# A shorter step table for the state-space heads: 43 steps in place of 45, at lower paces

## The reference, cut to what matters

```python
cs = jnp.cumsum(dA, axis=2)
lmat = segsum_exp(jnp.moveaxis(cs, 2, -1))            # exp(cs_i - cs_j), i >= j
cb = jnp.einsum('bclgn,bcsgn->bcgls', cm, bm)
y_diag = jnp.einsum('bcgls,bcgrls,bcsgrp->bclgrp', cb, lmat, xdt)
decay_states = jnp.exp(cs[:, :, -1:] - cs)
states = jnp.einsum('bclgn,bclgr,bclgrp->bcgrpn', bm, decay_states, xdt)
...
y_off = jnp.einsum('bclgn,bcgrpn,bclgr->bclgrp', cm, states_in, jnp.exp(cs))
return (y_diag + y_off).reshape(b, length, g, r, p)
```

```python
y = ssd_chunked(...) + xs_h * d_skip
y = y.reshape(b, length, SSM_D_INNER) * jax.nn.silu(z)
yg = y.reshape(b, length, SSM_GROUPS, SSM_NORM_GROUP)
yg = yg * lax.rsqrt(jnp.mean(yg * yg, axis=-1, keepdims=True) + RMS_EPS)
y_ssm = (yg * norm_w) @ w_out_ssm
```

## Time and profile before

| | |
|---|---|
| runs | 3578.57, 3582.47, 3583.49 us |
| profiled execution | 3578.57 us, span 3576.4 us, so 2.2 us lie around the span |
| instructions | 38935 |
| PE busy | 3362.9 us (94%) |
| PEld busy | 2729.3 us (76%) |
| DVE busy | 1723.0 us (48%) |
| ACT busy | 1340.7 us (37%) |
| mean granted PE clock | 0.973 |
| DMA | 288.05 MB, 81 GB/s on average |

### The profile page before, as it was taken

How to read it: one execution, slowest core, us unless ns; L and a number is a source line. 1 busy time by engine, 2 the same in 40 slices (tenths; PEclk the granted TensorE clock), 3 DMA queues, 4 the chain that set the end, 5 groups by cost and what they waited for, 6 DMA issues and landing times.

```text
span 3576.4 us, 38935 instructions
## 1 busy us (share of the span) xinstructions
PE 3362.9 (94%) x15366; PEld 2729.3 (76%) x15366; DVE 1723.0 (48%) x2415; ACT 1340.7 (37%) x1898; POOL 30.6 (1%) x62
## 2 busy tenths in 40 slices
PE   8999988799999999998888999999999998999998
PEld 6888765587888888876657788877777876778887
DVE  4443444654443444344555544455455566544443
ACT  4332334443332333233443333335454466433322
POOL 0000000000000000000000000000000000000000
PEclk9999999999999999999989999999999998999999
DMA  4333211112333232321211332321111222333332
GB/s 140 95 97 96 90 65 53 33 36 94 94 97 94 93 100 93 97 88 62 68 28 30 94 100 93 98 79 53 62 62 51 83 85 67 94 99 99 96 93 66
DMA packets 107396, 288.05 MB, mean 81 GB/s; under 512 B 22912, under 2 KB 34176, under 8 KB 107216
## 3 DMA queue, kind: packets, MB, share of 16 engines
q1 hardware_dynamic: 91696, 278.70, 24.9%
q10 hardware_dynamic: 14208, 2.63, 0.4%
q0 software_dynamic: 1312, 4.25, 0.4%
HBM read 282.64 MB, written 2.88 MB: 80 GB/s over the span
## 4 chain that ended last, share of the span: by engine, by line
PE 77%; DVE 11%; ACT 8%; issue 3%; DMA 1%; ACTq 0%; DVEq 0%; SPq 0%
PE ps L722 23%; PE ps L724 22%; PE ps L723 22%; DVE wl L1830 3%; ACT wh L1289 3%; DVE mf L2014 2%; PE ps L731 2%; PE ps L1029 1%; PE ps L1024 1%; PE ps L1185 1%; DVE mf L2024 1%; PE ps L736 1%; PE ps L1167 1%; PE ps L1181 0%; ACTq L1564 0%
## 5 line engine op out<-in xcount | busy, mean ns | idle before, releaser
L1830 DVE TENSOR_TENSOR wl<-raw,wh 128x1024 fp32r<-128x1024 f32 (+2 forms) x581 | 652.3, 1123 | 1421.9 <-ACT wh L1289 1420.2
L722 PE MATMUL ps<-hnh,wh 128*128 128x512 f32 x2712 | 1097.1, 405 | 40.9 <-DVE mf L2478 16.6
L723 PE MATMUL ps<-hnl,wh 128*128 128x512 f32 x2712 | 1071.6, 395 | 0.0
L724 PE MATMUL ps<-hnh,wl 128*128 128x512 f32 x2712 | 1070.9, 395 | 0.0
L1289 ACT ACTIVATE wh<-raw 128x1024 fp32r<-128x1024 f32 (+2 forms) x581 | 567.2, 977 | 1067.6 <-PE ps L724 1046.4
L722 PEld LDWEIGHTS ps<-hnh,wh 128*128 128x128 f32 x2712 | 520.6, 192 | 173.3 <-issue 25.2
L724 PEld LDWEIGHTS ps<-hnh,wl 128*128 128x128 f32 x2712 | 518.5, 191 | 111.6
L723 PEld LDWEIGHTS ps<-hnl,wh 128*128 128x128 f32 x2712 | 520.5, 192 | 109.0 <-issue 4.0
L722 PE MATMUL ps<-mr,wh 128*128 128x512 f32 x1300 | 512.4, 394 | 22.9 <-DVE h L1956 9.3
L724 PE MATMUL ps<-mr,wl 128*128 128x512 f32 x1300 | 507.4, 390 | 0.0
L723 PE MATMUL ps<-mr,wh 128*128 128x512 f32 x1300 | 507.3, 390 | 0.0
(11 more groups left out here) (324 smaller groups left out, 2537.9 us busy)
## 6 DMA issues: line engine op xcount, KB each, us to landing
raw<-in_w_in SPq DMA_DIRECT2D x140, 512.0 KB, 3.5
raw<-in_ffn_w_gate SPq DMA_DIRECT2D x88, 512.0 KB, 3.5
raw<-in_ffn_w_up SPq DMA_DIRECT2D x88, 512.0 KB, 3.5
raw<-in_ffn_w_down SPq DMA_DIRECT2D x64, 512.0 KB, 3.5
raw<-in_w_ffn_in SPq DMA_DIRECT2D x44, 512.0 KB, 3.5
raw<-in_ffn_w_down SPq DMA_DIRECT2D x32, 384.0 KB, 3.1
raw<-in_w_out SPq DMA_DIRECT2D x32, 256.0 KB, 2.7
raw<-in_w_out_ssm SPq DMA_DIRECT2D x32, 256.0 KB, 2.6
```

The lines of the kernel that those rows point to most:

```text
L722: self.e.matmul(out, ah, bh, start=start, stop=False, skip_group_check=shared)
L723: self.e.matmul(out, ah, bl, start=False, stop=False, skip_group_check=shared)
L724: m = self.e.matmul(out, al, bh, start=False, stop=stop, skip_group_check=shared)
L1830: self.e.tensor_tensor(lo[:, 0:n], k.raw[u % NRAW][:, 0:n], hi[:, 0:n].bitcast(F), ALU.subtract).then_inc(k.w_lo, 1)
```

## The change

The table of steps becomes two steps shorter and the four paces become lower, so that the steps still fill about the same blocks. The second pair of turns moves from step 10 to step 8. The arguments and all that follows from them move two steps forward (arguments 8 to 6, exponentials 9 to 7, `w` 10 to 8, values 14 to 12). The four x steps, which were 8, 9, 12 and 13, are 8, 9, 10 and 11. The states and the part between chunks move four steps forward (16 to 12), `y` and `z` two (18 to 16), root, diagonal and results two. The work itself, its instructions and their data, is the same.

```diff
-PACE_SSM_ROWS, PACE_SSM, PACE_LRU, PACE_LRU_END = 1.1, (1.15, 0.86, 0.86, 0.95), 0.65, 1.0
+PACE_SSM_ROWS, PACE_SSM, PACE_LRU, PACE_LRU_END = 1.1, (1.1, 0.82, 0.82, 0.9), 0.65, 1.0
...
-SSM_STEPS, SCAN_STEPS = 45, 11
-AT_CB, AT_TURN, AT_X = (0, 2, 2, 3), (6, 10), (8, 9, 12, 13)
-AT_ARG, AT_EXP, AT_W, AT_V = 8, 9, 10, 14
-AT_ST, AT_OFF, AT_Y = 16, 16, 18
-AT_ROOT, AT_RESULT, AT_HIGH, AT_LOW = (32, 34, 36), (39, 39, 39, 39), (40, 41, 42, 43), (41, 42, 43, 44)
+SSM_STEPS, SCAN_STEPS = 43, 11
+AT_CB, AT_TURN, AT_X = (0, 2, 2, 3), (6, 8), 8
+AT_ARG, AT_EXP, AT_W, AT_V = 6, 7, 8, 12
+AT_ST, AT_OFF, AT_Y = 12, 12, 16
+AT_ROOT, AT_RESULT, AT_HIGH, AT_LOW = (30, 32, 34), (37, 37, 37, 37), (38, 39, 40, 41), (39, 40, 41, 42)
...
-            four_at("x", AT_X), [(AT_ST + 2 + 4 * c, f"{n}{c}") for c in (1, 2) for n in "ds"],
+            [(AT_X + i, f"x{i}") for i in range(4)], [(AT_ST + 2 + 4 * c, f"{n}{c}") for c in (1, 2) for n in "ds"],
...
-            if t in AT_X:
-                i = AT_X.index(t)
+            if AT_X <= t < AT_X + 4:
+                i = t - AT_X
```

## The result

The changed kernel takes 3609.4 us (median of four, 3607.68 to 3610.8), the kernel before beside it 3580.74. The ratio is 1.0080, 95% interval 1.0062 to 1.0097. I had predicted 3597 us, +0.40%, with a range of 3584 to 3604. The sign was right, the size half of what came, and the time lies outside the range.

A forecast was written before the change was run, and what follows sets the result against it. PE bounds the kernel, nearly every instruction in the head groups being on the path. Added 19.25 us less removed 4.85 gave net +14.4: 3593.0 us for the profiled execution, 3597 as median (+0.40%), range 3584 to 3604.

The forecast's parts named there:

- the clock term: Behind turn 3's waits in groups 1 to 3, PE runs at lower clock: 3 x 1.65 = 4.95 us, bounds 0 and 7.
- turn 3 on x1, groups 1 to 3: PE waits at turn 3 for x1, now behind w0 on DVE: 3 x 3.2 = 9.7 us, plus 4.95 of clock.
- n0 on x3, groups 1 and 2: PE waits at n0 for x3, now behind a wl on DVE: 1.4 us twice, 2.8 us, no clock loss.
- turn 0 on CB, groups 2 and 3: Turn 0 stands one block nearer to ACT's copy of CB: 0.4 us in group 2, 0.8 in group 3.
- end of group 0: taking and diagonal: Results stand one block earlier, in front of a diagonal already 2.0 us late: 0.5 us added, bounds 0 and 1.4.
- removed: end of group 2: PE's wait for L2024 nearly goes, 2.3 us, with 1.65 us of lower clock: 3.95 us saved, bounds 0 and 4.1.
- removed: diagonal, groups 1 and 2: PE's waits for the diagonal go, as values end one block earlier before the results: 0.9 us saved.
- Rival 1: Added waits are there but absorbed by shrinking later waits: 3589 us, or 3584; chance 0.15.
- Rival 2: x1 comes early as in group 0, the added waits vanish and the removal remains: 3574 to 3578 us; chance 0.07.
- Rival 4: Results and product ends stay at the same blocks, all waits hide in slack: 3582 us, no change; chance 0.05.
- Rival 3: Longer waits: ACT's table switch costs more or the clock stays low longer: 3601 to 3606 us; chance 0.11.
- dearer switch on ACT: ACT's table switch costs more when nothing hides it, for example by a drain: 4 us in all.

The follow-up runs named there:

- e1: Changed kernel with x1 ahead of w0 and x3 ahead of the next wl on DVE (x steps 8, 8, 10, 10): 3588.17 us, ratio 1.0021.
- e9: Kernel before with only the second pair of turns at step 8 and x steps 8, 9, 10, 11: 3577.93 us, ratio 0.9999.
- e2: Changed kernel with the pace of group 0 alone back at 1.15 from 1.1: 3597.16 us, ratio 1.0047.
- e10: Changed table and x steps, with the kernel before's paces, 45 steps and results at step 39: 3588.91 us, ratio 1.0025.
- e5: Changed kernel with x steps 8, 8, 10, 10 and group 0 at a pace of 1.15: 3580.11 us, ratio 1.0002.
- e11: e5 with groups 0 and 3 pausing two steps ahead of the results and group 3 at pace 0.95: 3576.47 us, ratio 0.9987.
- e12: e11 with ACT's four scaled identities moved behind the copies of CB and B (step 4 in place of 0): 3569.97 us, ratio 0.9971.
- e6: e10 with x steps 8, 8, 10, 10, so x stands ahead of w: 3578.10 us, ratio 0.9995.
- e4: Kernel before with only the four paces of the changed kernel (1.1, 0.82, 0.82, 0.9): 3595.28 us, ratio 1.0041.
- e14: Changed kernel with 7 extra 128x512 matmuls on PE before the wait of turn 3 in groups 1 to 3: 3602.44 us, ratio 1.0058.
- e3: Changed kernel with 14 extra 128x512 matmuls on PE before the wait of turn 3 in groups 1 to 3: 3599.06 us, ratio 1.0053.

## Why the prediction was wrong

Two steps failed: the clock term, which was sized from one stretch and charged to one wait, and the wait for s2 in group 0, which was left out. In the order of its steps, with what the profiled executions show: idle time, and half of the busy time in the stretches at half clock. The small rows that are left out give 1.6 us of idle time back.

| step | predicted | idle | clock |
|---|---|---|---|
| turn 3 on x1, groups 1 to 3 | 9.7 + 4.95 | 9.7 | 8.3 |
| n0 on x3, groups 1 and 2 | 2.8 | 2.6 | 0 |
| turn 0 on CB, groups 2 and 3 | 1.2 | 1.4 | 1.7 |
| end of group 0: taking and diagonal | 0.5 | 1.6 | 2.0 |
| o3 and n1 on s2, group 0 | none | 4.2 | 1.6 |
| start of group 0 | none | -0.4 | 3.4 |
| removed: end of group 2 | -3.95 | -2.4 | -1.6 |
| removed: diagonal, groups 1 and 2 | -0.9 | -0.4 | 0 |

**Right:** the mechanism and its idle time. Turn 3 waits 3.22, 3.22 and 3.23 us (3.2 forecast), n0 1.28 twice (1.4), in the groups named, for the instructions named; the wait at the end of group 2 is gone with its clock. e1 confirms it by its removal, e9 by its condition: x1 has to stand behind a w0 that has to wait for the Silu's engine.

**Wrong, first: the clock term.** I priced the clock behind a wait of 3.2 us at 1.65, from the one row behind a wait of 2.42. That row was a case of 3.41 us at half clock, and I took it for the price. A wait of the right length stood in the same stage of the old trace:

```profile
2434.14 1.71 PE L736 MATMUL ps<-cst,mf 128*128 128x128 f32 x8 [3.25 <-ACT mf L1706]
```

It too had 3.41 us behind it, so this one row would have said the same. The whole trace says more: of PE's thirteen waits of 3.0 to 3.9 us in it, six have a stretch of 6.83 us, six one of 3.41, and one (3.02 us, at 1965.00) none. At 1.7 us for the short and 3.4 for the long ones that is 2.4 us on the mean, 7.1 for three waits: most of the price could have been read before the change. Turn 3 waited 3.2 us in seven cases (three in the changed kernel, two each in e2 and e10): the stretch at 0.50 was 3.41 us in two and 6.83 in five, 1.7 to 3.4 us lost, 2.8 on the mean. Three of them are 8.3 us where I had 4.95. And I charged the clock to turn 3 alone. The waits of the change on CB, at the end of group 0 and on s2 brought 5.3 us of it, where I had none. In all, the clock went from 5.1 to 20.5 us, and I had a net of 3.3.

**Wrong, second: group 0 was not read to its end.** The prediction compared DVE's order at the start of the groups and at the end of group 2. In group 0 the new table has o3 three blocks earlier, and the pace of 1.1 leaves s2, which o3 needs, behind the first taking: 3.8 us idle. The chain (buffer freed, `wh`, `wl`, taking, ACT's tap, DVE's tap, then d2 and s2) begins with the same parts as the one that I worked out for x3 from the earlier trace rows. The end of the group cost 3.6 us in place of 0.5. e2 took back the first whole and 2.6 us of the second.

3.4 us of clock at the start of group 0 I can't ascribe to the change: waits there are 2.0 and 2.8 us, before 2.1 and 3.3, and yet the half-clock stretches are 3.41 + 6.83 us in place of 3.41. e5 with the same list there has 6.83, e11 3.41 + 6.83, e12 with the shorter wait 3.41, and e9, whose lists up to there are those of the kernel before, 3.41 + 3.41. With one trace of each kernel it was not settled which of them an execution gets.

**The rivals.** Rival 1 (absorbed) is out: PE's waits grew by 14.7 us, and of those that were to stay only the small ones shrank, by 1.6. Rival 2 did not happen: x1 came 3.2 us after PE had reached turn 3. Rival 4 (no change) is out by the times. Rival 3, that the clock stays low longer, was the right one in kind, at 3601 to 3606 still too low. Its dearer switch on ACT was not seen: the load begins 0.01 us behind the Silu's end and takes 1.28 us, and the exponentials start 1.30 us behind its start, with PE and DVE both standing. The Trainium skill ("ScalarE: Activation LUTs", "What ACT_TABLE_LOAD costs") has a load of about 1283 ns and a drain about as long again. The load agrees with this trace, the drain does not.

## What to carry to other kernels

On an engine that is always busy, a wait has two prices, the idle time and the clock behind it; at turn 3, 3.2 us of idle cost 6.0 on the mean, and 1.6 us cost 1.6. Price both, and take the second from all waits of that length in the trace, not from one. Filling part of a wait can pay although nothing is done sooner: 7 empty matmuls in each of three waits made the changed kernel faster by some 7 us. It is the lesser remedy: with the waits removed (e1) it was 21.

When a table of steps and a pace change together, every group has to be compared to its last step. The order within a pair of steps that wait for different engines counts more than the number of steps: x ahead of w was worth 21 us, and once x was ahead, 45 steps at the old paces (e6, 0.9995) and 43 at the lower ones with group 0 at 1.15 (e5, 1.0002) were equal within the noise. A table and its paces belong together: the lower paces under the longer table cost 15 us (e4).

## What was not expected of the hardware

Waits of 1.6 to 1.9 us at turn 3 (three in e14, one in e2) had full clock behind them, those of 3.2 us (seven) had half clock in every case. Neither is a border that holds everywhere. The same wait of some 1.67 us at turn 0 of group 3 is followed by 3.41 us at half clock in the changed kernel and in e14, and not in e1, e2, e3, e4, e5 and e11. A wait of 2.41 or 2.42 us at the end of group 0 had a stretch behind it in the changed kernel and e1, and none in e3 and e14; one of 2.42 at the end of group 2 had it in the kernel before, one of 2.43 in e4 had none. And one wait of 3.02 us in the kernel before had none. What tips them stays open.
